# The weight split of a mixture-of-experts loop: one block in six moves from VectorE to GpSimd

## The reference

```python
def swiglu(xn, w_gu, w_down):
    g, u = jnp.split(xn @ w_gu, 2, axis=-1)
    return (jax.nn.silu(g) * u) @ w_down

def moe_swiglu(xn, router, w_gu, w_down):
    logits = (xn @ router).astype(jnp.float32)
    top_v, top_i = lax.top_k(logits, TOP_K)
    w = jax.nn.softmax(top_v, axis=-1)
    comb = jnp.sum(jax.nn.one_hot(top_i, N_EXPERTS, dtype=jnp.float32) * w[..., None],
                   axis=-2).astype(xn.dtype)
    out = jnp.zeros_like(xn)
    for e in range(N_EXPERTS):
        out = out + comb[..., e:e + 1] * swiglu(xn, w_gu[e], w_down[e])
    return out
```

## Time and profile before

| | |
|---|---|
| median of 3 runs | 2338.28 us |
| the profiled execution, its own time | 2345.53 us |
| its span in the profile | 2343.7 us |
| the experts' rounds, from the profile | about 642 to 1626 us, 56 rounds |
| PE busy / DVE busy / ACT busy / POOL busy, whole span | 98% / 76% / 58% / 5% |
| mean granted TensorE clock | 0.996 |

### The profile page before, as it was taken

One profiled execution on the slowest core, in us unless ns is written; L12 is line 12 of the kernel. 1 busy time (PEld: TensorE's weight loads), 2 busy tenths in 40 slices (PEclk: granted clock), 3 DMA queues, 4 the chain that ended last, 5 costly groups with the idle time before them and its releaser, 6 DMA issues.

```text
span 2343.7 us, 33405 instructions
## 1 busy us (share of the span) xinstructions
PE 2306.8 (98%) x14332; PEld 2061.4 (88%) x14332; DVE 1790.0 (76%) x1833; ACT 1367.1 (58%) x1354; POOL 122.8 (5%) x94
## 2 busy tenths in 40 slices
PE   9999999999999999999999999999999999999999
PEld 8989999899978888888887888888889999888999
DVE  6856556766788888888888888887777676777766
ACT  5435444465567677777776767766555444555342
POOL 2001001001100000000000000000310001301000
PEclk9999999999999999999999999999999999999999
DMA  8644455463499999999999999998334555433553
GB/s 267 203 144 163 162 202 176 136 217 125 162 352 367 350 349 347 367 351 349 345 364 345 357 346 361 372 348 292 117 109 144 194 188 169 132 123 112 189 171 109
DMA packets 309785, 566.87 MB, mean 242 GB/s; under 512 B 12482, under 2 KB 137697, under 8 KB 309504
## 3 DMA queue, kind: packets, MB, share of 16 engines
q1 hardware_dynamic: 304848, 559.34, 68.5%
q10 hardware_dynamic: 4784, 5.35, 0.7%
HBM read 563.60 MB, written 1.05 MB: 241 GB/s over the span
## 4 chain that ended last, share of the span: by engine, by line
PE 81%; DVE 8%; DMA 6%; ACT 4%; issue 0%; POOL 0%; ACTq 0%; SPq 0%; DVEq 0%; POOLq 0%
PE bank L1061 19%; PE bank L829 15%; PE bank L1079 10%; PE bank L669 8%; PE bank L813 7%; PE bank L657 6%; DMA raw<-in_od_moe_gu 5%; PE bank L256 5%; DVE wL L205 4%; ACT wH L234 2%; PE bank L681 2%; PE bank L1431 2%; PE bank L643 2%; DMA raw<-in_od_moe_down 1%; PE bank L1378 1%; DVE small L217 1%
## 5 line engine op out<-in xcount | busy, mean ns | idle before, releaser
L205 DVE TENSOR_TENSOR wL<-raw,wH 128x2048 fp32r<-128x2048 f32 (+4 forms) x550 | 1216.9, 2221 | 337.9 <-ACT wH L234 334.5
L234 ACT ACTIVATE wH<-raw 128x2048 fp32r<-128x2048 f32 (+4 forms) x550 | 1015.5, 1849 | 492.1 <-DMA raw<-in_od_moe_gu 119.0
L1061 PE MATMUL bank<-wH,ra 128*128 128x512 f32 x1792 | 578.9, 394 | 6.0 <-DVE wL L205 5.7
L1061 PEld LDWEIGHTS bank<-wH,ra 128*128 128x128 f32 x1792 | 336.4, 188 | 81.4 <-DVE wL L205 7.8
L829 PE MATMUL bank<-ra,wH 128*128 128x256 f32 x2112 | 382.4, 283 | 2.7 <-DVE arena L226 2.7
L1061 PE MATMUL bank<-wL,ra 128*128 128x512 f32 x896 | 348.8, 389 | 0.0
L829 PEld LDWEIGHTS bank<-ra,wH 128*128 128x128 f32 x2112 | 329.4, 192 | 4.5 <-DVE arena L226 3.5
L829 PE MATMUL bank<-ra,wL 128*128 128x256 f32 x1056 | 298.8, 283 | 0.0
L1079 PE MATMUL bank<-wH,ra 128*128 128x512 f32 x896 | 287.7, 392 | 0.9 <-DVE wL L205 0.9
L669 PE MATMUL bank<-wH,ra 128*128 128x512 f32 (+2 forms) x800 | 225.2, 359 | 0.5 <-DVE ra L208 0.5
L829 PEld LDWEIGHTS bank<-ra,wL 128*128 128x128 f32 x1056 | 202.7, 192 | 0.0
(11 more groups left out here) (212 smaller groups left out, 2524.6 us busy)
## 6 DMA issues: line engine op xcount, KB each, us to landing
raw<-in_od_moe_gu SPq DMA_DIRECT2D x224, 1024.0 KB, 6.9
raw<-in_od_moe_down SPq DMA_DIRECT2D x112, 1024.0 KB, 6.9
raw<-in_ev_ffn_gu SPq DMA_DIRECT2D x22, 1024.0 KB, 5.1
raw<-in_ffn_w_gate SPq DMA_DIRECT2D x22, 1024.0 KB, 5.5
raw<-in_ffn_w_up SPq DMA_DIRECT2D x22, 1024.0 KB, 5.4
raw<-in_ffn_w_down SPq DMA_DIRECT2D x22, 1024.0 KB, 5.0
raw<-in_xa_wkv SPq DMA_DIRECT2D x16, 1024.0 KB, 5.3
raw<-in_od_pw_w SPq DMA_DIRECT2D x12, 1024.0 KB, 5.1
```

What stands on the lines that cost most here:

```text
L205: self.op.tensor_tensor(out, a, b, op).then_inc(*self.sig.up(name))
L234: self.op.activation(out, a, ACT.Copy, **kw).then_inc(*self.sig.up(name))
L1061: m = p.op.matmul(out[:, :], a, b, start=half == 0 and c == 0 and i == 0, stop=half == 1 and c == 3 and i == 2)
```

## The change

GpSimd takes the low part of one block in each of the 56 rounds, up half 1. `pool_tags` names the blocks, `pool_block` waits for ScalarE's copy and does the same subtraction, `dve_blocks` leaves these blocks out, and `lower` gives TensorE and SyncE the semaphore to wait for.

```diff
+        self.by_pool = {self.index[tag] for tag in self.pool_tags()}
...
+    def pool_tags(self):
+
+        return [("moe", q // NRD, q % NRD, "up", 1) for q in range(NE * NRD)]
+
+    def lower(self, i):
+
+        return (self.pool if i in self.by_pool else self.dve).of(("w_lo", i))
+
+    def pool_block(self, g, *tag):
+
+        i = self.index[tag]
+        hi, lo = self.halves(i)
+        g.wait_ge(*self.act.of(("w_hi", i)))
+        g.tt(("w_lo", i), lo, self.raw_block(i), hi.bitcast(F32), ALU.subtract)
+
     def dve_blocks(self, v, tag):
 
         upto = min(self.index[tag] + 3, len(self.blocks))
         for i in range(self.dve_next, upto):
-            if self.blocks[i][2]:
+            if self.blocks[i][2] and i not in self.by_pool:
                 hi, lo = self.halves(i)
                 v.wait_ge(*self.act.of(("w_hi", i)))
                 v.tt(("w_lo", i), lo, self.raw_block(i), hi.bitcast(F32), ALU.subtract)
@@ pe_block
-        p.wait_ge(*self.dve.of(("w_lo", i)))
+        p.wait_ge(*self.lower(i))
@@ sync_program
-                    s.wait_ge(*self.dve.of(("w_lo", i - NR)))
+                    s.wait_ge(*self.lower(i - NR))
@@ pool_program
         self.pool_power(g, "m2", self.scm, ("m2", "mean"))
+        for tag in self.pool_tags():
+            self.pool_block(g, *tag)
```

## The result

The changed kernel takes 2427.57 us (median of 4 runs, 2423.91 to 2429.82), the kernel before 2340.19 (4 runs): ratio 1.0361, 95% interval 1.0345 to 1.0376, so 87 us slower. The direction was as forecast, the size was not: 2387 had been said, and 2427.57 stands at the very end of the range, 0.4 us inside it. It lies where the rival with the DMA ring had its prices (2415 for half of the rounds, 2443 for all).

The account below looks back on a forecast made before the run. TensorE, busy 977 of 984 us in the experts' stretch, was taken as the bound, with DMA at 98%. Stalls of 60.5 us less 11.4 of present waits added 49 to 2338.3, giving 2387; range 2351 to 2428.

Parts of the forecast that it names:

- the rival with the DMA ring: Landing in raw places stays at 7.72 us, adding 1.0 us a round: 2443, or 2415 for half the rounds; chance 0.12.
- VectorE's relief is worth nothing: 56 splits of 2.29 us leaving VectorE were costed at nothing; the most they could bring was 11.4 us.
- GpSimd's split takes 4.65 us: GpSimd's 2048-column split of up half 1, at 2.18 ns a column: 4.65 us, lower end 3.60.
- The rival with the faster rate: GpSimd at 1.66 ns a column splits in 3.60 us; kernel not slower, 2329 to 2340; chance 0.09.
- TensorE can't wait for it without a stall, 1.08 us a round, 60.5 in all: Before up half 1, TensorE's order and three wH places allow 3.57 us; a 4.65 us split stalls TensorE in 56 rounds.
- I let the 11.4 us of present waits be swallowed: TensorE's present waits for VectorE's splits vanish as longer rounds give DMA more time: 60.5 - 11.4 = 49 us.
- a single refill: Up half 1's raw place, freed 2.4 us later, takes next gate half 1: 0.2 us late, counted as nothing, 11 for range.
- A VectorE split stretched to 2.8 us, hidden: Down half 0's split waits some 0.7 us for GpSimd's lock, from 2.29 to about 2.8 us, 0.6 us to spare.
- GpSimd often waits for VectorE: GpSimd's split regularly delayed by up to 2.29 us behind a VectorE split; in a third of rounds 2431; chance 0.07.
- the forecast's own band: A GpSimd split of 4.3 to 5.0 us with nothing else: 2368 to 2407 us; chance 0.72.

Follow-up runs that it names:

- the six-place kernel before: The kernel before the change with six raw places instead of four in rounds 2 to 53: 2331.02 us, 0.9948.
- a split of 3.52 us: The changed kernel with GpSimd subtracting only the first 1536 of 2048 columns, four raw places kept: 2372.48 us, 1.0126.
- the six-place pair: The kernel before and the changed kernel, each with six raw places instead of four in rounds 2 to 53: 2331.02 and 2395.92 us.
- the fourth place: The changed kernel with a fourth place for wH and wL in rounds 42 to 53: 2419.86 us; with six raw places as well, 2383.05 us.
- The fills: The changed kernel with GpSimd's subtraction in rounds 2 to 53 replaced by fills of unused memory of about the same length: 2405.79 us, 1.0278.
- six raw places: The changed kernel with six raw places instead of four in rounds 2 to 53: 2395.92 us, 1.0230.

## Why the prediction was right, and where its size was off

- *VectorE's relief is worth nothing*: right. It lost 128 us of work, of which 60 came back as waiting for the lock, and the 11.4 us that could be had were the ring's, shown by the six-place kernel before.
- *GpSimd's split takes 4.65 us*: 4.60. The choice between the two rates of the earlier trace rows held; its reason, how the inputs lie, was not tested. The rival with the faster rate was wrong in another way: it gave 3.60 us and a kernel no slower than before, but with four raw places a split of 3.52 us cost 30 us.
- *TensorE can't wait for it without a stall, 1.08 us a round, 60.5 in all*: 1.14 to 1.16, 64.9 in all, as the six-place pair shows; the order of TensorE and the three `wH` places do it, as the fourth place shows. The missing 0.1 us a round has the size of the restart.
- *"I let the 11.4 us of present waits be swallowed"*: wrong, and this is the term that was mis-sized. The ring's part did not go from 11.4 to 0, it grew to 31.7. Forecast 60.5 - 11.4 = 49; measured 64.9 + 31.7 - 11.4 = 85, of the 87 observed (the 2 us left are within what the groups differ by). The reason given was that DMAs have more time in a longer round. But the ring is bound by the time around a place, not by the rate: the DMA share fell to 91% while landing stayed at a median of 7.0 us (6.9 before). My own count, three uses of a place in two rounds, came only with the experiments: with an estimated 11.75 us for one use in the slower rounds of before (the chain of waits from 1174 to 1251 us has 11.65 to 12.28), 3 x 11.75 + 2.3 = 37.6, so 18.8 a round, above the 17.87 of the path. That is no hard bound, as landing varies from 4.8 to 9.0 us, and behind the long rounds at the bounds of the experts (21 to 24 us) the ring had caught up: the next ones took 17.93 to 18.23. I had followed a single refill, on a good round, and found it 0.2 us late. In the slower rounds, which the trace of before had, the delay goes around.
- *A VectorE split stretched to 2.8 us, hidden*: it was stretched to up to 4.0, and the waits for the lock came to 60 us, 1.07 a round where 0.5 was forecast. Hidden from TensorE's next block, nearly always (its weight loads waited 1.7 us in all for VectorE); but it too delays refills. The fills put about 19 us on this and the clock together.
- *The ring rival* (chance 0.12) had the right place and, with half of the rounds, a price of 2415. Its reason was another, a landing of 7.72 us, where the median stayed at 7.0. It should have had the higher chance, since all it needed was the earlier trace rows and the later release that I had worked out myself.
- *GpSimd often waits for VectorE*: it did not, 4567 to 4614 ns.

The direction, the place of the stall and its price a round were understood. That the time still fell into the range was luck: the forecast's own band ended at 2407, 20 us below what was measured, and the upper edge of 2428 came from the rival.

The clock's part I can only read from the trace, not from an edit of its own. Summed in steps of 1 us over the experts, one minus the granted clock comes to 10 us in the changed kernel's profiled execution, and to nothing in before, six raw places or fills. The six rounds in which it fell are each 2.44 to 2.52 us longer than the same rounds with six raw places, 14.9 of the 31 us in all; the other 16 are spread over some 26 rounds. By the fills, some 13 of the 31.7 us are late refills alone and some 19 are lock and clock together. How these 19 divide remains open; the parts are coupled, as the clock fell only behind waits that the other two make.

## What to carry to other kernels

Before moving work from one engine to a slower one, ask for each buffer it touches how long the work may take there: here 3.45 us for `wH`/`wL` (three places) and, through `raw` (four places), less than VectorE already took, since the ring cost 11 us even before. In a loop like this one, where TensorE and the DMAs are both at 98%, follow a place of each ring of buffers over as many rounds as it takes to come back to the same block, and divide its time by the number of rounds; the ring with the longest time a round is what sets the pace. A busy engine that waits for its inputs, as VectorE did here, does not need help.

## What the runs showed of the hardware

TensorE's granted clock fell to half behind a stand of a few microseconds. The stretches view of the changed kernel around a wait of 2.70 us (columns as above, granted clock third from the end):

```profile
757.00:758.00 1.00, 0.01 (x1) 0.00 (x0) 0.18 (x1) 0.78 (x1) 1.00 (x1) 1.00 1.04 381
758.00:759.00 1.00, 0.00 (x0) 0.00 (x0) 1.00 (x1) 0.83 (x1) 1.00 (x1) 1.00 0.56 211
759.00:760.00 1.00, 0.29 (x1) 0.29 (x2) 1.00 (x1) 1.00 (x1) 0.65 (x1) 1.00 0.16 63
760.00:761.00 1.00, 1.00 (x5) 0.81 (x5) 1.00 (x1) 0.08 (x1) 0.00 (x0) 0.87 0.26 47
761.00:762.00 1.00, 1.00 (x3) 0.75 (x3) 1.00 (x2) 0.00 (x0) 0.00 (x0) 0.50 0.69 166
762.00:763.00 1.00, 1.00 (x4) 0.77 (x3) 1.00 (x1) 0.00 (x0) 0.00 (x0) 0.50 1.06 412
763.00:764.00 1.00, 1.00 (x4) 0.81 (x3) 1.00 (x1) 0.00 (x0) 0.00 (x0) 0.50 1.04 393
764.00:765.00 1.00, 1.00 (x5) 0.78 (x5) 0.64 (x2) 0.57 (x1) 0.00 (x0) 0.92 1.02 385
```

TensorE is idle to 759.71, runs, and from about 760.7 to 764.2 the clock is 0.50, that is 1.2 instead of 2.4 GHz, while it is busy again. This happened six times in the experts, each time within about 2 us of the end of a wait for GpSimd that the matmul rows show as 1.76 to 2.70 us, and took back about 1.7 us each (10 us / 6). It did not follow each such wait: behind 1.98 us at 666.84, 1.80 at 1282.91 and 1.95 at 1498.23 the clock stayed at 1.00. In the six-place kernel, whose waits are mostly 0.85 us, it never fell in the experts.

A VectorE split that waits for GpSimd's shows the wait as a longer instruction and not as idle time: 2.29 us became up to 4.02, and 60 us in all. Beside GpSimd's fills, which read no memory, it did not (2278 to 2295 ns).

GpSimd's two-input operations do not all go at one rate: the 1084 columns of the earlier trace rows went at 1.66 ns each, two operations of 256 columns with `smb` as an input took 0.64 us where another took 0.74, and the subtractions of 1536 to 2048 columns went at 2.15. That the shift by one column is the reason for the first was argued and not tested.
